# Second mixer's gates and output projections by token in 512 columns, and no filler matmuls at the opening

## The chip, the cores and the metric

One Trainium2 chip, one of its cores. The time is device microseconds of one execution, taken as the median of several runs.

## The reference

Two transformer blocks over 256 tokens of 1024 features, float32, one after the other. What the change touches is the end of the second block's mixer: three branches (a sparse attention `nsa`, a convolution, an attention over a memory), each projected to 1024 features and multiplied by its own gate, summed, and projected once more into the residual:

```python
xn = rms_norm_2(x, norm_mix)
proj = xn @ w_in                      # g_merge: the last 3 * 1024 columns
...
gm = jax.nn.sigmoid(g_merge).reshape(b, s, N_BRANCH, D_MODEL)
merged = gm[:, :, 0] * (o_nsa @ w_nsa_out) + gm[:, :, 1] * (u @ w_conv_out) + gm[:, :, 2] * (o_mem @ w_mem_out)
h = x + merged @ w_out
hn = rms_norm_2(h, norm_ffn)
return h + (silu(hn @ w_gate) * (hn @ w_up)) @ w_down
```

## The kernel before, in words

All weights (150 MB) are streamed once, in 143 chunks of 128x2048 float32 (1 MB). Every chunk passes through a ring of three buffers: SyncE's DMA writes `raw` (after the chunk three before has been split, semaphore `lo_made`), ScalarE casts it to float32r, `whi` (line 1295, `split_hi`, after TensorE has finished the chunk three before, `chunk_used`), VectorE subtracts the rounded from the raw one, `wlo` (line 1873, `split_lo`), and TensorE multiplies. Each product is three matmuls, hi*hi, hi*lo and lo*hi (`mm3`, lines 628 to 630), and the activations are held in two parts too, `hT_hi`/`hT_lo` and `oT_hi`/`oT_lo`. "Feature-major" is a result with features on the partitions and 256 tokens as columns (`feature_major`: weights stationary, activations moving, 256 columns a matmul); "by token" is one with 128 tokens on the partitions and 512 features as columns (`half_of_pair`, `into_residual`: activations stationary, weights moving, 512 columns a matmul). A pair's two halves are the first and last four of eight blocks of the contraction, accumulated in two banks of PSUM.

Each engine runs its own program, a loop over the chunks in which hand-written conditions on the step number `s` (0 at the chunk `kcvc`) say what else is done in that step. ScalarE's step for chunk n is: evacuate chunk n (`evac2`), cast chunk n+3 (`split_hi(n + RING)`, which waits until TensorE has finished chunk n), then pieces of attention. VectorE's is: evacuate an output chunk (`evac2_end`, lines 2237 and 2242), pieces of attention, `split_lo(n + RING)`, then a number of convolution taps given by the list `TAPS_AT` (line 2347). Units are the banks 4 and 5 of PSUM by turns; TensorE waits in `free_unit` until the one it wants has been drained.

The second mixer's chunks in order: `gm0..3` (memory gates), `gn0..3`, `gc0`, `ogn0,1`, `ogm0,1` (output projections, 512 columns each), `gc1..3`, `ogc0,1`, `xout0..3` (`w_out_2`, into the residual). A gate chunk is 256 features, feature-major; ScalarE evacuates it with a tanh (line 1607) once it is finished. An output chunk is feature-major too, in two units, and VectorE multiplies each unit by its gate (line 2237) and adds it to the merged tile `Mg` (line 2242, semaphore `merged`). The merged tile lies as `xout` wants it, so ScalarE (line 1805, `mhi_made`) and VectorE (line 2449, `mlo_made`) only split it in two parts. TensorE's attention pieces stand behind a step's chunk: `att_values(s - 11)`, `att_turn(s - 10)`, `att_scores(s - 8)`. The convolution's layer norm is at steps 26 to 28: sums on TensorE (lines 1230, 1235), the rest on ScalarE (lines 1791 to 1799, 1728 to 1742) and VectorE (lines 2435 to 2442, 2373, 2430).

At the opening TensorE multiplies the identity by itself (`keep_warm`, line 748), 4 matmuls and then 10, with a small transpose of the norm's gains between them (line 922), until the rows of x have been scaled; then `turn_input` (line 772) turns x into feature-major form with 16 matmuls. A float32 matmul of the identity counts as two instructions in the trace.

## Time and profile before

| | |
|---|---|
| median of 3 runs | 910.32 us (910.21 to 910.83) |
| the profiled execution | 910.42 us, its span 908.4 us |
| TensorE busy | 901.1 us, 99% of the span |
| its weight loads | 800.8 us, 88% |
| VectorE, ScalarE, GpSimd | 69%, 57%, 9% |
| granted TensorE clock | 1.00 |
| HBM read | 153.5 MB, 170 GB/s over the span |

Every duration below comes from the profiled execution, whose span begins at 0 and leaves 2.0 us of its time outside. Matmuls overlap their neighbours, so that a chunk's length is read from the start of its first matmul to the start of the next chunk's first. DVE is VectorE, ACT is ScalarE, PE is TensorE and PEld its weight loads.

### The profile page before, as it was taken

The numbers are of one execution on the slowest core, as the hardware profiler recorded it, in microseconds if no ns is written. First come the engines' busy times: TensorE is split into PE (matmuls) and PEld (weight loads), VectorE is DVE, ScalarE is ACT, GpSimd is POOL, SyncE is SP. The second block draws the span as 40 slices with busy tenths as digits, with TensorE's granted clock in tenths as the row PEclk, the third lists the DMA queues.
The fourth block names the chain that finished last, engine by engine and source line by source line (L and its number), as shares of the span: only waits on it lengthen the run. The fifth ranks groups of instructions, "written<-read, shape, count | busy, mean of one in ns | idle before, by whom it ended". The sixth has DMA issues, their size and how long they took to land.

```text
span 908.4 us, 14119 instructions
## 1 busy us (share of the span) xinstructions
PE 901.1 (99%) x5682; PEld 800.8 (88%) x5682; DVE 629.4 (69%) x805; ACT 518.6 (57%) x731; POOL 78.4 (9%) x145
## 2 busy tenths in 40 slices
PE   8999999999999999999999999999999999999998
PEld 7888888999989888888889988888999888888887
DVE  5646576766776666566685889888878586666664
ACT  6646666765455444444476777877365564444441
POOL 8603342020010000000000000000000000000000
PEclk9999999999999999999999999999999999999999
DMA  9654333466545555555555863433445475556541
GB/s 275 219 188 159 114 123 108 142 225 212 181 163 168 204 185 185 185 186 189 200 149 166 259 189 100 139 124 110 139 140 185 139 230 188 185 186 193 187 173 46
DMA packets 115672, 155.35 MB, mean 171 GB/s; under 512 B 2649, under 2 KB 94913, under 8 KB 115618
## 3 DMA queue, kind: packets, MB, share of 16 engines
q1 hardware_dynamic: 114704, 151.57, 51.4%
q0 software_dynamic: 864, 2.98, 1.0%
q8 instruction: 39, 0.64, 0.3%
q14 instruction: 15, 0.12, 0.0%
q10 hardware_dynamic: 50, 0.04, 0.0%
HBM read 153.53 MB, written 1.05 MB: 170 GB/s over the span
## 4 chain that ended last, share of the span: by engine, by line
PE 95%; ACT 2%; DVE 2%; issue 1%; DMA 0%; ACTq 0%; DVEq 0%
PE PS L628 19%; PE PS L629 18%; PE PS L630 18%; PE PS L987 15%; PE PS L992 8%; PE PS L681 3%; PE PS L687 1%; PE PS L1123 1%; PE PS L1101 1%; PE PS L891 1%; ACT whi L1295 1%; PE PS L1035 1%; DVE wlo L1873 1%; PE PS L1159 1%; PE PS L842 1%
## 5 line engine op out<-in xcount | busy, mean ns | idle before, releaser
L1873 DVE TENSOR_TENSOR wlo<-raw,whi 128x2048 fp32r<-128x2048 f32 x141 | 323.8, 2297 | 124.5 <-ACT whi L1295 123.1
L1295 ACT CAST whi<-raw 128x2048 fp32r<-128x2048 f32 x141 | 269.0, 1908 | 112.7 <-PE PS L630 109.5
L628 PE MATMUL PS<-hT,whi 128*128 128x256 f32 (+1 forms) x504 | 145.2, 288 | 0.0
L987 PE MATMUL PS<-hT,whi 128*128 128x512 f32 x608 | 144.7, 390 | 0.0
L630 PE MATMUL PS<-hT,wlo 128*128 128x256 f32 (+1 forms) x504 | 142.5, 283 | 0.0
L629 PE MATMUL PS<-hT,whi 128*128 128x256 f32 (+1 forms) x504 | 142.5, 283 | 0.0
L987 PEld LDWEIGHTS PS<-hT,whi 128*128 128x128 f32 x608 | 113.1, 188 | 23.1 <-issue 0.2
L628 PEld LDWEIGHTS PS<-hT,whi 128*128 128x128 f32 (+1 forms) x504 | 96.0, 190 | 0.7 <-DVE wlo L1873 0.4
L629 PEld LDWEIGHTS PS<-hT,whi 128*128 128x128 f32 (+1 forms) x504 | 96.0, 191 | 0.2
L630 PEld LDWEIGHTS PS<-hT,wlo 128*128 128x128 f32 (+1 forms) x504 | 96.0, 190 | 0.0
L628 PE MATMUL PS<-whi,aT_hi 128*128 128x512 f32 x216 | 84.3, 391 | 0.0
L629 PE MATMUL PS<-wlo,aT_hi 128*128 128x512 f32 x216 | 84.3, 390 | 0.0
L630 PE MATMUL PS<-whi,aT_lo 128*128 128x512 f32 x216 | 84.0, 389 | 0.0
L992 PEld LDWEIGHTS PS<-hT,wlo 128*128 128x128 f32 x608 | 78.0, 191 | 3.0
L992 PE MATMUL PS<-hT,wlo 128*128 128x256 f32 x608 | 78.9, 283 | 0.0
L628 PE MATMUL PS<-oT_hi,whi 128*128 128x256 f32 x224 | 64.1, 286 | 1.0 <-DVE AR L2142 0.5
L629 PE MATMUL PS<-oT_lo,whi 128*128 128x256 f32 x224 | 63.4, 283 | 0.0
L630 PE MATMUL PS<-oT_hi,wlo 128*128 128x256 f32 x224 | 63.4, 283 | 0.0
L628 PE MATMUL PS<-whi,hT 128*128 128x512 f32 (+1 forms) x160 | 61.7, 386 | 0.0
L630 PE MATMUL PS<-whi,hT 128*128 128x512 f32 (+1 forms) x160 | 60.7, 379 | 0.0
L629 PE MATMUL PS<-wlo,hT 128*128 128x512 f32 (+1 forms) x160 | 60.6, 379 | 0.0
L2347 DVE SCALAR_TENSOR_TENSOR AR<-AR,cw 128x256 f32<-128x256 f32 x120 | 49.0, 480 | 0.1
(381 smaller groups left out, 1342.9 us busy)
## 6 DMA issues: line engine op xcount, KB each, us to landing
raw<-in_w_in_dram SPq DMA_DIRECT2D x47, 1024.0 KB, 5.2
raw<-in_w_ff_dram SPq DMA_DIRECT2D x32, 1024.0 KB, 5.2
raw<-in_w_gate_dram SPq DMA_DIRECT2D x11, 1024.0 KB, 5.2
raw<-in_w_up_dram SPq DMA_DIRECT2D x11, 1024.0 KB, 5.3
raw<-in_w_down_dram SPq DMA_DIRECT2D x11, 1024.0 KB, 5.0
raw<-in_w_out_dram SPq DMA_DIRECT2D x8, 1024.0 KB, 5.0
raw<-in_w_proj_gla_dram SPq DMA_DIRECT2D x4, 1024.0 KB, 5.1
raw<-in_w_mem_kv_dram SPq DMA_DIRECT2D x4, 1024.0 KB, 5.1
```

The costliest lines, as they stand in the source:

```text
L628: pe.matmul(dst, a_hi, b_hi, start=start, stop=False, skip_group_check=True)
L629: pe.matmul(dst, a_hi, b_lo, start=False, stop=False, skip_group_check=True)
L630: return pe.matmul(dst, a_lo, b_hi, start=False, stop=stop, skip_group_check=True)
L681: pe.matmul(PS[:, b + c, :], w_hi[:, k, c * P:(c + 1) * P], hT[:, k, :, :].rearrange("p w t -> p (w t)"), start=k == 0, stop=False, skip_g ...
L687: mm = pe.matmul(PS[:, b + c, 0:T], w_lo[:, k, c * P:(c + 1) * P], hT_hi[:, k, :], start=False, stop=k == KT - 1, skip_group_check=True)
L842: pe.matmul(PS[:, b, 0:384], negtri[:, :], sbt[:, b, 1, :], start=False, stop=False, skip_group_check=True)
L891: pe.matmul(o, QK[:, l, :], q, start=True, stop=True)
L987: pe.matmul(PS[:, bank + c, :], w_hi[:, k, c * P:(c + 1) * P], hT[:, k, :, :].rearrange("p w t -> p (w t)"), start=k == 0, stop=False, ski ...
L992: mm = pe.matmul(PS[:, bank + c, 0:T], w_lo[:, k, c * P:(c + 1) * P], hT_hi[:, k, :], start=False, stop=k == KT - 1, skip_group_check=True)
L1295: act.copy(whi[:, n % RING, :], raw[:, n % RING, :]).then_inc(hi_made, 1)
L1873: dve.tensor_tensor(wlo[:, n % RING, :], raw[:, n % RING, :], whi[:, n % RING, :].bitcast(F32), ALU.subtract).then_inc(lo_made, 1)
L2347: ins = dve.scalar_tensor_tensor(cacc[:, f, :], src, cw[:, f, k:k + 1], cacc[:, f, :], ALU.mult, ALU.add)
```

## The change

The twelve gate chunks become six pairs by token (`gm0`+`gm1` and so on; each half is now 512 features and half of the contraction), `gc1` moves from behind `ogm1` to directly behind `gc0`, the gates are laid out by token in other places, and the first of a pair is evacuated at the end of ScalarE's step, once the second half of the pair has finished its first bank. Output chunks are computed by token (`out_by_token`). The merged tile is now by token, so TensorE turns it (`turn_merged`, 8 transposes in the middle of `ogc1`, 8 behind `xout0`), into banks 6 and 7, from which ScalarE (`merged_hi`) and VectorE (`merged_lo`) take their parts. `keep_warm` and its two calls go. The diff, with the declarations and the tables of loads cut:

```diff
     for name in ("gm", "gn"):
-        for c in range(4):
-            gate_chunk(name, c)
-    gate_chunk("gc", 0)
+        for c in (0, 2):
+            gate_pair(name, c)
+    gate_pair("gc", 0)
     for name in ("gn", "gm"):
             out_chunk(name, c)
-    for c in range(1, 4):
-        gate_chunk("gc", c)
+    gate_pair("gc", 2)
     for c in range(2):
...
-            c = int(name[2])
-            if name[1] == "m":
-                return Mg[:, 2 * c:2 * c + 2, :]
-            c = c - 1 if name[1] == "c" else c
-            flat = AR[:, 8312:8824] if c < 0 else AR[:, 7800:8312] if c == 3 else relu[:, c, :]
-            return flat.rearrange("p (f t) -> p f t", f=2)
+            kind, j = name[:2], int(name[2])
+            if kind == "gm":
+                return xn[:, j % 2, 512 * (j // 2):512 * (j // 2) + 512]
+            if kind == "gn":
+                return relu[:, j, :] if j < 3 else AR[:, 7800:8312]
+            return (AR[:, 8312:8824], AR[:, 5120:5632], relu[:, 1, :], relu[:, 2, :])[j]
...
         units_before_ffn1 = unit_of["vm0"]
-        FIRST_OF_PAIR = ("sbv0", "gv0", "gout0", "gv2", "gout2", "vm0")
-        SECOND_OF_PAIR = ("sbv1", "gv1", "gout1", "gv3", "gout3", "vm1")
+        GATES = [f"{kind}{c}" for kind in ("gm", "gn", "gc") for c in range(4)]
+        FIRST_OF_PAIR = ["sbv0", "gv0", "gout0", "gv2", "gout2", "vm0"] + GATES[0::2]
+        SECOND_OF_PAIR = ["sbv1", "gv1", "gout1", "gv3", "gout3", "vm1"] + GATES[1::2]
         TWO_BANKS = [name for name in at if name.startswith(("projs", "o")) or name in SECOND_OF_PAIR]
...
-            def keep_warm(bank, count):
-
-                for _ in range(count):
-                    pe.matmul(PS[:, bank, 0:P], ident[:, :], ident[:, :], start=True, stop=True)
-
             def transposes(event, q, src):
...
             pe.wait_ge(ident_made, 4)
-            keep_warm(7, 4)
             pe.wait_ge(prm0_in, 16)
             pe.transpose(PS[:, 5, 0:8], prm_rows[0:8, :], ident[0:8, 0:8]).then_inc(prm_tr, 1)
-            keep_warm(7, 10)
             pe.wait_ge(prm0_made, 1)
...
+            def turn_merged(c):
+
+                pe.wait_ge(merged, 4 + 2 * c + 2)
+                if c == 1:
+                    pe.wait_ge(mlo_made, 2)
+                for f in range(4):
+                    for a in range(TT):
+                        mm = pe.transpose(PS[:, 6 + f // 2, f % 2 * T + a * P:f % 2 * T + (a + 1) * P],
+                                          xn[:, a, 512 * c + f * P:512 * c + (f + 1) * P], ident[:, :])
+                    if f % 2 == 1:
+                        mm.then_inc(mtr_made, 1)
+
+            def out_by_token(name, k0):
+
+                n, u = at[name], unit_of[name]
+                take(n)
+                w_hi, w_lo = parts(n, 512)
+                for a in range(TT):
+                    if (name, a) == ("ogc1", 1):
+                        turn_merged(0)
+                    free_unit(u + a)
+                    for k in range(4):
+                        mm = mm3(lin(u + a), oT_hi[:, k0 + k, a * P:(a + 1) * P], oT_lo[:, k0 + k, a * P:(a + 1) * P],
+                                 w_hi[:, k, :], w_lo[:, k, :], k == 0, k == 3)
+                    if a == 0:
+                        mm.then_inc(bank_full, 1)
+                mm.then_inc(chunk_used, 1)
+
             B2 = at["kcvc"]
...
                             pe.wait_ge(att_lo, 4)
-                    feature_major(name, oT_hi, oT_lo, (8, 4, 0)[br], 4, 512)
+                    out_by_token(name, (8, 4, 0)[br])
+                elif name in GATES:
+                    half_of_pair(name, hT_hi, hT_lo)
                 else:
...
                               start=c == 0, by_token=c == 3)
+                if c == 0:
+                    turn_merged(1)
             turn_sums()
...
                 n, u = at[name], unit_of[name]
-                if name == "vm0":
-                    act.wait_ge(bank_full, TWO_BANKS.index("vm1") + 1)
+                if name in FIRST_OF_PAIR:
+                    act.wait_ge(bank_full, TWO_BANKS.index(f"{name[:2]}{c_of(name) + 1}") + 1)
                 else:
...
                 elif name[0] == "g":
-                    if name in ("gc1", "gc2", "gc3"):
+                    if name in ("gc2", "gc3"):
                         act.wait_ge(merged, c_of(name))
-                    act.activation(gate_tile(name), two, ACT.Tanh, scale=0.5).then_inc(done, 1)
+                    act.activation(gate_tile(name), lin(u), ACT.Tanh, scale=0.5).then_inc(done, 1)
                 elif name[:2] == "cg":
...
+            def merged_hi(c):
+                for q in (2 * c, 2 * c + 1):
+                    act.wait_ge(mtr_made, q + 1)
+                    act.activation(hT_hi[:, 2 * q:2 * q + 2, :], PS[:, 6 + q % 2, :].rearrange("p (f t) -> p f t", f=2),
+                                   ACT.Copy, scale=0.5).then_inc(mhi_made, 1)
+
             V1 = at["vm0"]
...
                     turned_hi(3, hT_hi, G_MIX2)
-                if name[0] != "o" and name not in ("vm0", "wk0", "wv0"):
+                if name[0] != "o" and name not in FIRST_OF_PAIR and name not in ("wk0", "wv0"):
                     evac2(name)
...
                     tables(EXP_TANH)
-                if name in ("ogc0", "ogc1"):
-                    c = int(name[3])
-                    for i in range(2):
-                        act.wait_ge(merged, 4 + 2 * c + i + 1)
-                        q = 2 * c + i
-                        act.activation(hT_hi[:, 2 * q:2 * q + 2, :], Mg[:, 2 * q:2 * q + 2, :], ACT.Copy,
-                                       scale=0.5).then_inc(mhi_made, 1)
+                if name in GATES and name in FIRST_OF_PAIR:
+                    evac2(name)
+                if name == "ogc1":
+                    merged_hi(0)
+            merged_hi(1)
             for c in range(3):
...
                             dve.wait_ge(chunk_used, at[name] + 1)
-                        f = slice(4 * c + 2 * i, 4 * c + 2 * i + 2)
                         d = drained[(u + i) % 2]
-                        two = lin(u + i).rearrange("p (f t) -> p f t", f=2)
-                        m, t = Mg[:, f, :], gate_tile(f"{name[1:3]}{2 * c + i}")
+                        m, t = gate_tile(f"gm{2 * c + i}"), gate_tile(f"{name[1:3]}{2 * c + i}")
                         g = m if name[2] == "m" else t
-                        dve.scalar_tensor_tensor(g, g, 1.0, two, ALU.add, ALU.mult).then_inc(d, 1)
+                        dve.scalar_tensor_tensor(g, g, 1.0, lin(u + i), ALU.add, ALU.mult).then_inc(d, 1)
                         if name[2] == "n":
...
+            def merged_lo(c):
+                for q in (2 * c, 2 * c + 1):
+                    dve.wait_ge(mhi_made, q + 1)
+                    dve.scalar_tensor_tensor(hT_lo[:, 2 * q:2 * q + 2, :], PS[:, 6 + q % 2, :].rearrange("p (f t) -> p f t", f=2),
+                                             0.5, hT_hi[:, 2 * q:2 * q + 2, :].bitcast(F32), ALU.mult,
+                                             ALU.subtract).then_inc(mlo_made, 1)
+
             def taps_by(s):
...
                 evac(name)
+                if name == "ogc1":
+                    merged_lo(0)
                 if name[0] == "o":
...
                                              ALU.mult).then_inc(cv_y, 1)
-                if name in ("ogc0", "ogc1"):
-                    c = int(name[3])
-                    for i in range(2):
-                        q = 2 * c + i
-                        dve.wait_ge(mhi_made, q + 1)
-                        dve.scalar_tensor_tensor(hT_lo[:, 2 * q:2 * q + 2, :], Mg[:, 2 * q:2 * q + 2, :], 0.5,
-                                                 hT_hi[:, 2 * q:2 * q + 2, :].bitcast(F32), ALU.mult,
-                                                 ALU.subtract).then_inc(mlo_made, 1)
+            merged_lo(1)
             for c in range(2):
```

Three places where instructions move. In the rows, a tile's name stands left of the arrow where it is written, and the names in brackets are the semaphores waited for; line numbers are each kernel's own.

ScalarE at the end of the mixer, before: the evacuations of `gc2` and `gc3` (relu), the casts of whi for `ogc1`, `xout0`, `xout1`, `xout2`, `xout3` and the chunk behind it, and the two pairs of copies that split the merged tile (xn).
```order
L1607 ACTIVATE relu<-PS 128x512 [waits merged,chunk_used]
L1295 CAST whi<-raw 128x2048 [waits chunk_used,landed0]
L1607 ACTIVATE relu<-PS 128x512 [waits merged,chunk_used]
L1295 CAST whi<-raw 128x2048 [waits chunk_used,landed1]
L1295 CAST whi<-raw 128x2048 [waits chunk_used,landed2]
L1805 ACTIVATE hT<-xn 128x2x256 [waits merged] x2
L1295 CAST whi<-raw 128x2048 [waits chunk_used,landed0]
L1805 ACTIVATE hT<-xn 128x2x256 [waits merged] x2
L1295 CAST whi<-raw 128x2048 [waits chunk_used,landed1]
L1295 CAST whi<-raw 128x2048 [waits chunk_used,landed2]
```
And now (the second row is the cast for `ogc1`; the three rows ahead of the copies are the casts for `xout0`, `xout1` and `xout2`):
```order
L1771 ACTIVATE oT_hi<-AR 128x1024 [waits cv_f]
L1319 CAST whi<-raw 128x2048 [waits chunk_used,landed0]
L1631 ACTIVATE relu<-PS 128x512 [waits merged,bank_full]
L1631 ACTIVATE relu<-PS 128x512 [waits merged,chunk_used]
L1319 CAST whi<-raw 128x2048 [waits chunk_used,landed1]
L1319 CAST whi<-raw 128x2048 [waits chunk_used,landed2]
L1319 CAST whi<-raw 128x2048 [waits chunk_used,landed0]
L1738 ACTIVATE hT<-PS 128x2x256 [waits mtr_made] x4
L1319 CAST whi<-raw 128x2048 [waits chunk_used,landed1]
L1319 CAST whi<-raw 128x2048 [waits chunk_used,landed2]
```
All four copies now stand together behind the third of these casts, and they wait for TensorE's turning; before, the first two stood ahead of it.

VectorE where the taps end, before: the taps of steps 23, 24 and 25 (`gc0`, `ogn0`, `ogn1`), with the gate products of `ogn0` and `ogn1` (relu and AR) between them.
```order
L2347 SCALAR_TENSOR_TENSOR AR<-AR,cw 128x256 [waits taps] x7
L2237 SCALAR_TENSOR_TENSOR relu<-relu,PS 128x512 [waits bank_full]
L2237 SCALAR_TENSOR_TENSOR relu<-relu,PS 128x512 [waits chunk_used]
L1873 TENSOR_TENSOR wlo<-raw,whi 128x2048 [waits hi_made]
L2320 TENSOR_TENSOR oT_lo<-PS,oT_hi 128x4x128 [waits att_hi]
L2347 SCALAR_TENSOR_TENSOR AR<-AR,cw 128x256 [waits taps] x6
L2237 SCALAR_TENSOR_TENSOR relu<-relu,PS 128x512 [waits bank_full]
L2237 SCALAR_TENSOR_TENSOR AR<-AR,PS 128x512 [waits chunk_used]
L1873 TENSOR_TENSOR wlo<-raw,whi 128x2048 [waits hi_made]
L2347 SCALAR_TENSOR_TENSOR AR<-AR,cw 128x256 [waits taps] x5
L2237 SCALAR_TENSOR_TENSOR xn<-xn,PS 128x512 [waits bank_full]
```
And now, steps 23 to 26 (`gc0`, `gc1`, `ogn0`, `ogn1`):
```order
L2373 SCALAR_TENSOR_TENSOR AR<-AR,cw 128x256 [waits taps] x7
L1901 TENSOR_TENSOR wlo<-raw,whi 128x2048 [waits hi_made]
L2346 TENSOR_TENSOR oT_lo<-PS,oT_hi 128x4x128 [waits att_hi]
L2373 SCALAR_TENSOR_TENSOR AR<-AR,cw 128x256 [waits taps] x6
L2263 SCALAR_TENSOR_TENSOR relu<-relu,PS 128x512 [waits bank_full]
L2263 SCALAR_TENSOR_TENSOR relu<-relu,PS 128x512 [waits chunk_used]
L1901 TENSOR_TENSOR wlo<-raw,whi 128x2048 [waits hi_made]
L2373 SCALAR_TENSOR_TENSOR AR<-AR,cw 128x256 [waits taps] x5
L2263 SCALAR_TENSOR_TENSOR relu<-relu,PS 128x512 [waits bank_full]
L2263 SCALAR_TENSOR_TENSOR AR<-AR,PS 128x512 [waits chunk_used]
```
The six taps stood behind the products of `ogn0`; they now stand ahead of them, in the step of `gc1`.

TensorE at the opening, before:
```order
L748 MATMUL PS<-ident 128x128 [waits ident_made]
L748 MATMUL PS<-ident 128x128 x3
L922 MATMUL PS<-ident,AR 128x8 [waits prm0_in]
L748 MATMUL PS<-ident 128x128 x10
L772 MATMUL PS<-AR,res 128x128 [waits rdiag_made,prm0_made]
L772 MATMUL PS<-AR,res 128x128 x5
L772 MATMUL PS<-AR,res 128x128 [waits rdiag_made]
L772 MATMUL PS<-AR,res 128x128 x9
L628 MATMUL PS<-hT,whi 66x256 [waits trlo_made,lo_made]
```
And now:
```order
L915 MATMUL PS<-ident,AR 128x8 [waits prm0_in,ident_made]
L766 MATMUL PS<-AR,res 128x128 [waits rdiag_made,prm0_made]
L766 MATMUL PS<-AR,res 128x128 x5
L766 MATMUL PS<-AR,res 128x128 [waits rdiag_made]
L766 MATMUL PS<-AR,res 128x128 x9
L627 MATMUL PS<-hT,whi 66x256 [waits trlo_made,lo_made]
```
The two runs of the identity are gone; what stands behind them waits for the same semaphores as before.

## Rows read from the trace of the kernel before

**Rows 1.** The page, part 1: busy us (share of the span) and instructions of each engine
```profile
PE 901.1 (99%) x5682; PEld 800.8 (88%) x5682; DVE 629.4 (69%) x805; ACT 518.6 (57%) x731; POOL 78.4 (9%) x145
```

**Rows 2.** Waits of TensorE over the whole span: us in total, times, longest us
```profile
PE PS L628 <- DVE AR L2142: 0.5, 1, 0.5
PE PS L628 <- DVE relu L2237: 0.5, 1, 0.5
```

**Rows 3.** Timeline of TensorE, first matmuls of ogc0, ogc1, xout0, xout1 (start us, us)
```profile
686.99 0.28 PE L628 MATMUL PS<-oT_hi,whi 128*128 128x256 f32 x1
...
692.75 0.28 PE L628 MATMUL PS<-oT_hi,whi 128*128 128x256 f32 x1
...
698.51 0.40 PE L628 MATMUL PS<-whi,hT 128*128 128x512 f32 x1
...
703.98 0.39 PE L628 MATMUL PS<-whi,hT 128*128 128x512 f32 x1
```

**Rows 4.** Busy us (and instructions) of PE, PEld, DVE, ACT, POOL, gm1 to gc0
```profile
568.47:638.04 69.57, 69.57 (x545) 62.03 (x544) 59.73 (x125) 53.41 (x117) 0.00 (x0) 1.00 0.41 129
```

**Rows 5.** Timeline of TensorE, eight transposes inside the first block (start us, us)
```profile
247.71 1.04 PE L756 MATMUL PS<-ident,AR 128*128 128x128 f32 x8
248.51 0.47 PE L628 MATMUL PS<-whi,hT 128*128 128x512 f32 x1
```

**Rows 6.** Timeline of ScalarE after the end of ogc1
```profile
698.77 1.92 ACT L1295 CAST whi<-raw 128x2048 fp32r<-128x2048 f32 x1 [2.80 <-PE PS L630]
700.58 0.62 ACT L1805 ACTIVATE hT<-xn 128x512 fp32r<-128x512 f32 x1
```

**Rows 7.** Timeline of VectorE, during ogc1
```profile
697.16 1.28 DVE L2449 SCALAR_TENSOR_TENSOR hT<-xn,hT 128x512 fp32r<-128x512 f32 x2
```

**Rows 8.** The chain of waits, 640 to 720 us (start us, us, what)
```profile
646.55 1.91 ACT whi L1295
648.48 2.29 DVE wlo L1873
...
651.37 2.37 DVE AR L2347 x6
653.75 0.61 DVE relu L2237
654.49 0.36 PE PS L628
...
668.15 1.73 PE PS L1235 x8
```

**Rows 9.** Timeline of ScalarE after the end of gc0
```profile
638.08 0.60 ACT L1607 ACTIVATE AR<-PS 128x512 f32<-128x512 f32 x1 [1.35 <-PE PS L630]
638.57 1.89 ACT L1295 CAST whi<-raw 128x2048 fp32r<-128x2048 f32 x1
```

**Rows 10.** Timeline of TensorE, between ogn0 and ogn1
```profile
646.29 1.95 PE L1142 MATMUL PS<-TMP,AR 128*128 128x128 f32 x16
648.00 0.36 PE L628 MATMUL PS<-oT_hi,whi 128*128 128x256 f32 x1
```

**Rows 11.** Timeline of VectorE, the convolution after ogm1
```profile
673.78 1.22 DVE L2442 SCALAR_TENSOR_TENSOR AR<-AR 128x1024 f32<-128x1024 f32 x1
```

**Rows 12.** Timeline of TensorE, opening (start us, us)
```profile
1.91 2.08 PE L748 MATMUL PS<-ident 128*128 128x128 f32 x8 [1.91 <-POOL eps L520]
...
4.12 3.29 PE L748 MATMUL PS<-ident 128*128 128x128 f32 x20
7.89 3.81 PE L772 MATMUL PS<-AR,res 128*128 128x128 f32 x32 [0.47 <-DVE AR L2079]
```

**Rows 13.** The same, two pieces of the fillers, merged by narrower windows
```profile
4.49 1.47 PE L748 MATMUL PS<-ident 128*128 128x128 f32 x6
...
5.91 1.50 PE L748 MATMUL PS<-ident 128*128 128x128 f32 x12
```

**Rows 14.** Timeline of VectorE, opening
```profile
7.18 0.55 DVE L2079 TENSOR_SCALAR AR<-ident,stat 128x128 f32<-128x128 f32 x1
```

More of the change, by code:

```diff
@@ L91, in key_chunk, with gate_pair @@
         chunk(name, cols(w_in_2, 768, 512).rearrange("p k (b h n) -> p k b h n", b=2, h=2)[:, :, :, c, :])
-    def gate_chunk(name, c):
-        chunk(f"{name}{c}", cols(w_in_2, {"gm": g20, "gc": g10, "gn": g00}[name] + CW * c))
+    def gate_pair(name, c):
+        pair(name, w_in_2, {"gm": g20, "gc": g10, "gn": g00}[name], c)
     def out_chunk(name, c):
@@ L268, in two_block_kernel @@
         hwork = AR[:, 9150:9210]
-        Mg = xn[:, :, :].rearrange("p a (f t) -> p (a f) t", t=T)
         fsq, qsq = xn[:, 0, 0:512], xn[:, 0, 512:1024]
@@ L344, in two_block_kernel @@
                              "cv_sig", "cv_f", "cv_hi", "cv_lo"))
-        merged, mhi_made, mlo_made = sem("merged"), sem("mhi_made"), sem("mlo_made")
+        merged, mtr_made, mhi_made, mlo_made = sem("merged"), sem("mtr_made"), sem("mhi_made"), sem("mlo_made")
         act_link = sem("act_link")
```

## The prediction

> **What bounds the kernel now.** I read the page first: TensorE is busy 901.1 of 908.4 us [rows 1]. Then its idle time: 1.9 us before the first instruction and 0.5 before the turning of x [rows 12]; the two largest waits after the opening are 0.5 us each [rows 2]. So the time is the sum of TensorE's work, and a change counts in three ways: shorter work, added work, and new waits for the other engines. In the third view, the busy times of the stretch with gates and attention, VectorE has 59.7 and ScalarE 53.4 of 69.6 us [rows 4]; they keep up with little to spare, so their order has to be read too. Last I read the opening in the timeline. What a measurement of this kernel can tell from no change is taken as 0.2%, 1.8 us.
>
> **Shorter work.** Twelve gate chunks and six output chunks of the second mixer go from 48 matmuls of 256 columns to 24 of 512. An old chunk lasts 5.76 us, from the first matmul of ogc0 to that of ogc1 and again to xout0; xout0, which already has 24 matmuls of 512, lasts 5.47 [rows 3]. Eighteen times 0.3 is 5.2 to 5.8 us; I take **-5.6**, as xout0's length contains one slow start. The widest bound below would be nothing gained, which the equal product of columns (48 x 256 = 24 x 512) would allow; the rows 3 exclude it.
>
> **Added work.** Two times eight transposes of the merged tile. Eight of the same size cost 0.80 us up to the next matmul, which then takes 0.08 more than usual [rows 5]. Twice 0.9 is **+1.8** (1.6 to 2.1).
>
> **New wait before xout0.** TensorE used to read the split of a tile that was merged long before. Now the chain is transposes in PSUM, ScalarE's copy, VectorE's subtraction, xout0. The order of ScalarE (shown above) has both pairs of copies behind the cast of xout2, and that cast waits until ogc1 is finished, since it writes the buffer that ogc1 reads. So from the moment at which xout0 starts today (698.51) nothing is hidden: 0.26 until the cast starts, 1.81 from there to the next instruction, a copy 0.62 [rows 3, 6], 0.03 until VectorE takes it, one of the two subtractions 0.68 [rows 7], and 0.15 from VectorE's end to TensorE's start, as from 7.73 to 7.89 [rows 12, 14]. Sum 3.55, with 0.05 for a slow first matmul **+3.6** (3.0 if the hand-overs overlap, 4.2 if reading PSUM is slower). The eight transposes themselves stand before ogc1's second half, where they need ogc0's merge; by the same steps that is ready about 1 us early. The second turn stands after xout0 and has its whole 5.4 us for VectorE's four merge operations, and xout1 is between it and its reader: nothing.
>
> **New wait at ogn1.** The chain of waits shows that the old order is already tight in one place: after ogn0 the cast (646.55), the subtraction, six taps (651.37) and VectorE's read of ogn1's bank (653.75) end only at 654.49, where TensorE had waited 0.50 us [rows 8, 2]. That cast to that read is one step. Now the step belongs to gc1, which is the second of its pair, so ScalarE first evacuates it, 0.49 us ahead of the cast [rows 9]; and the bank that VectorE reads behind the taps is ogn0's, which ogn1 needs. From the end of gc1: 0.04 until ScalarE begins, 0.49, and 7.94 (646.55 to 654.49) = 8.5 us until ogn1 may start. TensorE arrives after 1.71 us of memory attention [rows 10] and ogn0's 5.45: 7.2. It waits 1.3; the old 0.5 goes. **+0.8** (0.3 to 1.3).
>
> **New wait at gc2.** The convolution's normalisation ran beside a gate chunk; now it runs beside ogm1, an output chunk, whose first bank VectorE reads only behind it. VectorE is through at 675.00, 6.85 us after 668.15 [rows 8, 11]; plus 0.61 and 0.15 is 7.6. TensorE needs 1.73 for its sums [rows 8] and 5.45: 7.2. A wait also costs the overlap of two neighbouring matmuls, so **+0.4** (0 to 0.6).
>
> **The rest of the mixer.** The first half of a gate pair is evacuated in the middle of the second, so both banks of a pair come free before the next pair only if ScalarE has by then left the attention's exponentials. Its work per step is only moved from the start of a step to its end, and two evacuations follow each other where the pair ends; the next pair starts behind 2 to 4 us of attention matmuls. VectorE's idle time in that stretch, 9.8 us [rows 4], absorbs the 0.3 us that each step gets shorter. I count nothing, with 1 us as the upper bound if that cover goes. DMA sees the same bytes and stands ahead of the casts.
>
> **The opening.** The fillers run from 1.91 to 7.4 us; the turning of x starts at 7.89 and waits for VectorE's 7.18 + 0.55, not for them [rows 12, 14]. Removing them frees no time. But six passes of the filler from 4.49 on last 1.47 us, twelve from 5.91 on only 1.50 [rows 13]: less one pass's own 0.40 and 0.28, that is 0.213 against 0.111 us each, so TensorE left its lower level (1.2 GHz) for the upper (2.4 GHz) at about 5.8, after 3.9 us of fillers. (The granted clock reads 1.00 in every row; here the pace tells.) The turning of x, 32 passes in 3.81 us, ran wholly at the upper level. Without fillers TensorE stands still until 7.9 but for one tiny transpose. If the level follows the work, 3.9 us at the lower level give 3.9 x (1 - 0.111/0.213) = **+1.9**; nothing hides it, as TensorE never waits for long later. Bounds: nothing, if the level rises with time and not with work; 2.6, if it needs as much as the whole 5.5 us that the fillers gave it. One rise cannot tell which.
> The Trainium skill ("TensorE: Matmul & The Clock Gate", What's actually happening) says that the throttled state is the default and that activity releases it. By that rule the opening costs its 1.9 us and the total is the forecast; by the other reading the total is rival 1.
>
> **Sum.** -5.6 + 1.8 + 3.6 + 0.8 + 0.4 + 1.9 = +2.9 us, against the profiled execution's 910.4 (span 908.4): 913.3, span 911.3. The median of the runs is 0.1 below the profiled one: **913.2 us**, 0.32% slower.
>
> **Rivals.**
> 1. The opening is free: the clock would have risen by then anyway. For: the trace shows one rise only. Against: the engine was working whenever it rose. 910.3 + 1.0 = 911.3, no measurable change. It decides once the opening costs under 0.8 us.
> 2. The clock falls in the 3.6 us before xout0. The trace has no such idle stretch once TensorE is warm, so nothing in it excludes this. Coming back would cost once more what the fillers needed, 1.9: 915.1.
> The Trainium skill warns of just that (same page, Why this matters for your kernels): an idle gap between bursts of matmuls puts the gate back to half. No stretch of this trace shows it.
> 3. Faster: the copies of the merged tile reach ScalarE before ogc1 ends. Copy, subtraction and hand-overs, 1.5 us, then hide behind ogc1's second half of 2.7, and the wait before xout0 is gone: with a free opening 910.3 - 5.6 + 1.8 + 0.8 + 0.4 = 907.7, with the opening paid 909.6. It decides when that wait is under 0.8 us and the opening free. Against it stands ScalarE's order, which a trace can hardly contradict.
> 4. TensorE outruns ScalarE and VectorE all along the gates, each pair waiting for its banks, say 0.5 us for each of six pairs: 3 us more, 916.2.
>
> **Chances.** Forecast 0.60, rival 1 0.18, rival 2 0.10, rival 3 0.08, rival 4 0.04. The forecast's own spread puts 0.09 of its 0.60 below 912.1, and of rival 3 0.03 are with the opening paid, 909.6. Slower by over 0.2%: 0.51 + 0.10 + 0.04 = 0.65. Within 0.2% (908.5 to 912.1): 0.09 + 0.18 + 0.03 = 0.30. Faster: 0.05. The range for 8 in 10 reaches from rival 1 (911.3, less 0.4 for its terms) to rival 2 (915.1): 910.9 to 915.3. All bounds together give 909.4 (-5.8 + 1.6 + 3.0 + 0.3) to 916.9 (-5.2 + 2.1 + 4.2 + 1.3 + 0.6 + 1.0 + 2.6).
>
> **What would show it.** In the changed kernel's profile: gate and output chunks 5.45 apart; TensorE's waits list VectorE's subtraction ahead of xout0 with about 3.4 (counted from the end of the matmul before), VectorE's gate product ahead of ogn1 with 1.3 and of gc2 with 0.3; turning x takes 5.7 us instead of 3.8. I am wrong if the turning of x lasts 3.8, if the wait before xout0 is under 1, if the matmuls of xout0 are twice as long as before, or if TensorE waits for ScalarE's gate evacuations.

## The result, and the profile after

The changed kernel takes 914.92 us in the median of 5 runs (914.28 to 917.20), the kernel before 910.32 in the 5 runs beside it (910.11 to 911.83): a ratio of 1.0052, with a 95% interval of 1.0040 to 1.0064. It is 4.6 us slower, where 2.9 were forecast. Measured a second time (the last experiment) it was 6.0 slower, which is outside the forecast's range. The profiled execution took 914.28 us, span 912.5, so 4.1 more span than before.

The page of the changed kernel, part 1, which answers to [rows 1]:

```profile
span 912.5 us, 13226 instructions
PE 896.0 (98%) x5238; PEld 776.4 (85%) x5238; DVE 629.8 (69%) x805; ACT 519.1 (57%) x731; POOL 72.6 (8%) x145
```

TensorE's work fell by 5.1 us and the span grew by 4.1, so 9 us of new idle time have to be found. They stand in TensorE's waits of the changed kernel (for what it waited, us in total, times, longest; PS L766 <- DVE AR L2107 is a write to PSUM in line 766 that waited for VectorE's write to AR in line 2107); compare [rows 2]:

```profile
PE PS L766 <- DVE AR L2107: 3.8, 1, 3.8
PE PS L915 <- DMA AR<-in_norm_mix_dram: 3.3, 1, 3.3
PE PS L627 <- DVE hT L2380: 3.3, 1, 3.3
PE PS L627 <- DVE relu L2263: 1.2, 1, 1.2
PE PS L627 <- DVE AR L2170: 0.5, 1, 0.5
PE PS L627 <- DVE xn L2263: 0.4, 1, 0.4
```

The first two rows are the opening, where fillers used to run. The third is the new wait ahead of `xout0`, the fourth the one at `ogn1`, the sixth the one at `gc2`. The 0.5 is an old wait in the first mixer.

**The wait ahead of `xout0`.** Timelines of the changed kernel (start us, us, engine, line, operation, count, and in brackets the idle time before it and what ended it), first of ScalarE:

```profile
696.97 1.90 ACT L1319 CAST whi<-raw 128x2048 fp32r<-128x2048 f32 x1 [4.76 <-PE PS L629]
698.77 1.08 ACT L1738 ACTIVATE hT<-PS 128x512 fp32r<-128x512 f32 x2
```

of VectorE:

```profile
699.40 1.29 DVE L2380 SCALAR_TENSOR_TENSOR hT<-PS,hT 128x512 fp32r<-128x512 f32 x2 [4.86 <-ACT hT L1738]
```

and of TensorE:

```profile
696.49 0.39 PE L629 MATMUL PS<-whi,oT_lo 128*128 128x512 f32 x1
700.14 0.80 PE L627 MATMUL PS<-whi,hT 128*128 128x512 f32 x1 [3.26 <-DVE hT L2380]
700.74 0.63 PE L628 MATMUL PS<-wlo,hT 128*128 128x512 f32 x1
701.16 0.63 PE L629 MATMUL PS<-whi,hT 128*128 128x512 f32 x1
...
703.51 0.40 PE L629 MATMUL PS<-whi,hT 128*128 128x512 f32 x1
703.75 0.40 PE L627 MATMUL PS<-whi,hT 128*128 128x512 f32 x1
```

ScalarE stood idle for 4.76 us in front of a cast that could not start until `ogc1` had ended, and the two copies that `xout0` needs stood behind that cast: the chain of the prediction, link by link. Two things more are in these rows. The first matmuls of `xout0` are 0.42 us apart, the later ones 0.23. And the windows of the changed kernel (PE, PEld, DVE, ACT and POOL busy; then the granted clock, the DMA share and GB/s) show why:

```profile
690.00:697.00 7.00, 6.82 (x33) 5.26 (x32) 4.39 (x5) 1.95 (x2) 0.00 (x0) 1.00 0.58 200
697.00:700.20 3.20, 0.06 (x1) 0.06 (x1) 0.80 (x2) 2.85 (x3) 0.00 (x0) 0.94 0.62 219
700.20:703.20 3.00, 3.00 (x7) 2.42 (x8) 2.93 (x5) 0.00 (x0) 0.00 (x0) 0.50 0.00 0
703.20:707.00 3.80, 3.80 (x18) 3.05 (x18) 2.33 (x2) 0.00 (x0) 0.00 (x0) 1.00 0.07 12
```

Behind 3.26 us in which TensorE did nothing, the granted clock is 0.50 (1.2 GHz) for three microseconds of full work. That is rival 2, to which the prediction had given 0.10. It is also one of the prediction's own signs of being wrong, the matmuls of `xout0` twice as long as before: up to 703.28 they are nearly that, with 0.41 to 0.43 us from one start to the next (0.60 behind the very first) against 0.23.

**The chunks.** First matmuls of `gc3`, `ogc0` and `ogc1`, and the two turnings of the merged tile, in the changed kernel; compare [rows 3, 5]:

```profile
679.16 0.39 PE L627 MATMUL PS<-whi,hT 128*128 128x512 f32 x1
...
684.60 0.39 PE L627 MATMUL PS<-whi,oT_hi 128*128 128x512 f32 x1
...
690.27 0.47 PE L627 MATMUL PS<-whi,oT_hi 128*128 128x512 f32 x1
...
693.08 1.04 PE L1164 MATMUL PS<-ident,xn 128*128 128x128 f32 x8
...
707.18 1.03 PE L1164 MATMUL PS<-ident,xn 128*128 128x128 f32 x8
707.97 0.48 PE L627 MATMUL PS<-whi,hT 128*128 128x512 f32 x1
```

`gc3` lasts 5.44 (684.60 - 679.16) instead of 5.76. The eight transposes hold TensorE for 0.79 (707.18 to 707.97).

**The opening.** TensorE in the changed kernel, against [rows 12]:

```profile
3.27 0.24 PE L915 MATMUL PS<-ident,AR 8*128 8x8 f32 x1 [3.27 <-DMA AR<-in_norm_mix_dram]
7.35 5.23 PE L766 MATMUL PS<-AR,res 128*128 128x128 f32 x32 [3.84 <-DVE AR L2107]
12.34 0.36 PE L627 MATMUL PS<-hT,whi 128*66 128x256 f32 x1
```

The turning of x begins 0.5 earlier and lasts 5.2 instead of 3.8 us. The clock's column doesn't show why, but the number of matmuls in two windows of 2 us does (11 and 19, with the column at 1.00 in both):

```profile
8.00:10.00 2.00, 2.00 (x11) 2.00 (x11) 1.27 (x4) 0.53 (x1) 1.76 (x4) 1.00 1.10 349
10.00:12.00 2.00, 2.00 (x19) 2.00 (x18) 0.75 (x2) 1.33 (x4) 1.62 (x6) 1.00 1.09 346
```

A good mark for what the whole opening costs is the matmul behind the 0.5 wait in the first mixer, because everything up to it is the same work: 213.37 before, here 214.31.

```profile
214.31 0.36 PE L627 MATMUL PS<-oT_hi,whi 128*128 128x256 f32 x1 [0.51 <-DVE AR L2170]
```

So of the 4.1 us of span 0.9 are the opening and 3.2 the second mixer.

### The profile page after: what moved, and what is told of

Same layout as the page of the kernel before. It is cut to its first block, busy times and chain, and to the rows that moved or that the text cites. A ratio compares the mean times of both kernels' runs of the same rounds, so it can differ in the third digit from the quotient of the medians.

```text
span 912.5 us, 13226 instructions
## 1 busy us (share of the span) xinstructions
PE 896.0 (98%) x5238; PEld 776.4 (85%) x5238; DVE 629.8 (69%) x805; ACT 519.1 (57%) x731; POOL 72.6 (8%) x145
## 4 chain that ended last, share of the span: by engine, by line
PE 94%; ACT 3%; DVE 2%; issue 1%; DMA 0%; ACTq 0%; DVEq 0%
PE PS L627 18%; PE PS L629 18%; PE PS L628 18%; PE PS L979 15%; PE PS L984 8%; PE PS L680 3%; PE PS L686 1%; ACT whi L1319 1%; PE PS L1115 1%; PE PS L1093 1%; PE PS L885 1%; PE PS L1027 1%; DVE wlo L1901 1%; PE PS L1151 1%; PE PS L766 1%
## 5 line engine op out<-in xcount | busy, mean ns | idle before, releaser
L627 PE MATMUL PS<-whi,hT 128*128 128x512 f32 (+1 forms) x256 | 100.9, 394 | 3.7 <-DVE hT L2380 3.3
L629 PE MATMUL PS<-whi,hT 128*128 128x512 f32 (+1 forms) x256 | 98.7, 386 | 0.0
L628 PE MATMUL PS<-wlo,hT 128*128 128x512 f32 (+1 forms) x256 | 98.5, 385 | 0.0
L627 PE MATMUL PS<-hT,whi 128*128 128x256 f32 (+1 forms) x312 | 90.1, 289 | 0.0
L628 PE MATMUL PS<-hT,whi 128*128 128x256 f32 (+1 forms) x312 | 88.2, 283 | 0.0
L629 PE MATMUL PS<-hT,wlo 128*128 128x256 f32 (+1 forms) x312 | 88.2, 283 | 0.0
L627 PEld LDWEIGHTS PS<-whi,hT 128*128 128x128 f32 x256 | 48.5, 190 | 13.3 <-DVE hT L2380 3.7
L627 PEld LDWEIGHTS PS<-hT,whi 128*128 128x128 f32 (+1 forms) x312 | 59.2, 190 | 0.6 <-DVE wlo L1901 0.4
L628 PEld LDWEIGHTS PS<-hT,whi 128*128 128x128 f32 (+1 forms) x312 | 59.2, 190 | 0.2
L629 PEld LDWEIGHTS PS<-hT,wlo 128*128 128x128 f32 (+1 forms) x312 | 59.2, 190 | 0.0
L629 PEld LDWEIGHTS PS<-whi,hT 128*128 128x128 f32 x256 | 48.4, 189 | 9.9
L628 PEld LDWEIGHTS PS<-wlo,hT 128*128 128x128 f32 x256 | 48.6, 190 | 8.9
```

What stands on the lines that cost most here:

```text
L627: pe.matmul(dst, a_hi, b_hi, start=start, stop=False, skip_group_check=True)
L628: pe.matmul(dst, a_hi, b_lo, start=False, stop=False, skip_group_check=True)
L629: return pe.matmul(dst, a_lo, b_hi, start=False, stop=stop, skip_group_check=True)
```

## The experiments

Each kernel below is the changed one with the edit shown, unless it says otherwise. "Mark" is that matmul of the first mixer in its profile, less 213.37. The change in the first row has the 5 runs of the kernel before given above. Of the ten kernels below it, the first four ran on one chip beside 21 runs of the kernel before, the next four on another with 28 runs to compare (median 910.57 for both), and the last two on a third beside 15 runs with 911.0. So differences between rows of different groups can be off by some tenths of a us.

| kernel | median us (runs) | ratio, 95% interval | span | mark | waits: `xout0`, `ogn1` |
|---|---|---|---|---|---|
| the change | 914.92 (5) | 1.0052 (1.0040 to 1.0064) | 912.5 | +0.9 | 3.3, 1.2 |
| fillers back | 914.11 (5) | 1.0036 (1.0023 to 1.0050) | 912.4 | +0.6 | 3.3, 1.2 |
| before, without fillers | 912.77 (11) | 1.0022 (1.0013 to 1.0031) | 911.5 | +3.0 | 0, 0.5 |
| copies first | 910.75 (11) | 1.0000 (0.9991 to 1.0009) | 908.7 | +2.1 | 0, 1.2 |
| fill the wait | 914.34 (5) | 1.0041 (1.0028 to 1.0055) | 912.2 | +2.1 | 0.6 + fillers, 1.2 |
| fillers back, copies first | 908.30 (9) | 0.9974 (0.9964 to 0.9984) | 906.7 | +0.1 | 0, 1.2 |
| the same, taps moved | 908.35 (8) | 0.9974 (0.9963 to 0.9984) | 907.0 | +0.6 | 0, 0 |
| fillers back, fill the wait | 911.98 (11) | 1.0015 (1.0006 to 1.0024) | 910.1 | 0.0 | 0.6 + fillers, 1.2 |
| copies first, taps moved | 911.17 (11) | 1.0001 (0.9992 to 1.0010) | 909.5 | +3.1 | 0, 0 |
| the change again | 916.98 (5) | 1.0071 (1.0057 to 1.0085) | 914.2 | +2.3 | 3.3, 1.2 |
| four fillers only, copies first | 911.16 (11) | 1.0000 (0.9991 to 1.0009) | 909.6 | +3.0 | 0, 1.2 |

### Fillers back

```diff
             pe.wait_ge(ident_made, 4)
+            keep_warm(7, 4)
             pe.wait_ge(prm0_in, 16)
...
+            keep_warm(7, 10)
             pe.wait_ge(prm0_made, 1)
```

> The changed kernel with both runs of fillers back at the opening. Theory (each part of the change has its own price): the turning of x runs at the full level again, 32 passes in 3.8 us instead of 5.2, and the profiled span loses the 0.9 us that the opening cost in the profile, up to 3 in executions whose clock rose later; median 912 to 914, about 1.5 us above nothing but the mixer's part (+3.2). Rival (the fillers cost or give nothing, the spread of the changed kernel comes from elsewhere): median unchanged at 914.9, and as wide a spread, 3 us.

It brought only 0.8 us in the median. In its profile the rise of the clock came later than in the profile of before, so the mark is still 0.6 late; the wait ahead of `xout0` and the half level are there as in the change. Its opening, TensorE and then VectorE:

```profile
4.12 4.50 PE L747 MATMUL PS<-ident 128*128 128x128 f32 x20
8.45 3.74 PE L771 MATMUL PS<-AR,res 128*128 128x128 f32 x32
```
```profile
6.90 0.35 DVE L2114 TENSOR_SCALAR AR<-ident,stat 128x128 f32<-128x128 f32 x1
```

The second run of fillers lasts 4.5 us here, against 3.3 in [rows 12], and ends over a microsecond after VectorE has made what the turning needs (7.25). So fillers are not free: when the clock rises late, they hold up the work behind them. In the four profiled kernels with all 14 of them the turning starts at 7.88, 8.09, 8.45 and 8.54. By itself this run could not price the opening; the pairs below do.

### The kernel before, without fillers

```diff
-            keep_warm(7, 4)
...
-            keep_warm(7, 10)
```

> The kernel before without its fillers, nothing else changed. Theory: +0.9 us as in the profile of the changed kernel, to +3 in executions whose clock rises later; median 911.2 to 912.5 and a wider spread than before's own. Rival (clock rises with time, not with work): 910.3 and a turning of x of 3.8 us.

2.2 us slower, and no wait of the second mixer is touched, so the opening is not free: rival 1 falls. The mark is 3.0 late. Of this, 1.3 stand as a new wait among TensorE's waits of this kernel, and the timelines of ScalarE and of SyncE, which issues the transfers, say where it is from:

```profile
PE PS L681 <- DVE AR L1987: 1.3, 1, 1.3
```
```profile
25.82 1.91 ACT L1293 CAST whi<-raw 128x2048 fp32r<-128x2048 f32 x1 [3.69 <-DMA raw<-in_w_in_dram]
```
```profile
19.29 0.39 SPq L466 DMA_DIRECT2D raw<-in_w_in_dram  x1
```

The same cast (of `sbk1`, the fourth chunk after `low`) starts at 22.55 in the kernel before, there too behind the DMA of its weights, which is issued at 17.16:

```profile
17.16 0.39 SPq L466 DMA_DIRECT2D raw<-in_w_in_dram  x1
```

So of the 3.3 us by which the cast is later, 2.1 come from the issue: it waits until VectorE has split the chunk whose buffer it overwrites, and the late opening delays that. The other 1.2 are the transfer, 6.5 us from issue to cast instead of 5.4. The new wait occurs in three of the seven profiled kernels without all 14 fillers (marks 3.0 to 3.1) and not in the other four (0.9 to 2.3). In three of those four the issue is just as late (19.20 to 19.40), but the cast starts at 24.57 to 24.90. What makes the transfer longer in the first three, no run shows.

### Copies first

```diff
+                if name == "ogc1":
+                    merged_hi(0)
                 split_hi(n + RING)
...
-                if name == "ogc1":
-                    merged_hi(0)
             merged_hi(1)
```

> The changed kernel with ScalarE's first pair of copies of the merged tile ahead of the cast of xout2. Theory: transposes done, copy and subtraction take 1.3 us and hide behind ogc1's second half of 2.7, so the wait of 3.3 before xout0 goes, and with it the fall of the clock that follows it (1.5): 4.9 less in the profile, median about 910.2, no TensorE wait on VectorE's subtraction above 0.3. Rival (the wait is set by VectorE's queue or the cast itself comes late for xout2): 2 us or less of it goes, median 912.5 to 913.

The wait ahead of `xout0` is gone, and with it the half level: 4.2 us less than the change, for two lines that change places. The span is 3.8 less with an opening 1.2 later, so the mixer gives back 5.0, where 4.9 were expected. ScalarE and VectorE in this kernel:

```profile
694.91 1.09 ACT L1738 ACTIVATE hT<-PS 128x512 fp32r<-128x512 f32 x2 [1.54 <-PE PS L1164]
698.16 1.92 ACT L1319 CAST whi<-raw 128x2048 fp32r<-128x2048 f32 x1 [2.17 <-PE PS L629]
```
```profile
695.60 1.28 DVE L2380 SCALAR_TENSOR_TENSOR hT<-PS,hT 128x512 fp32r<-128x512 f32 x2
```

The copies now fill idle time of ScalarE, and both subtractions end at 696.88, 1.2 us before `ogc1` does (698.07). The cast is not delayed, because it waits for TensorE in either order. The price of the whole chain was its place in a queue, not its length.

### Fill the wait

```diff
+            keep_warm(3, 12)
             for c in range(4):
                 pe.wait_ge(mlo_made, c + 1)
```

> The changed kernel with 12 matmuls of the identity into an unused bank between ogc1 and xout0, where TensorE waits 3.3 us. They take 24 passes of 0.11, 2.7 us, so the wait for VectorE stays as a rest of about 0.6. Theory (an idle stretch lets the clock fall, at a price of its own): granted clock 1.00 through xout0, xout0 5.5 instead of 7.0 us long, median 1 to 1.5 below the changed kernel, 913.5. Rival (the price is the wait alone and the fall is an accident of the profile): no change, 914.9.

The time between `ogc1` and `xout0` stays as long and the clock stays up. Against copies first, whose mark is the same (+2.1), the span is 3.5 us longer: that is the wait without its effect on the clock. Against the change the median is only 0.6 lower, between what the theory and its rival named, but this profile's opening is 1.1 us later, so these two do not compare well; the kernel with the fillers back and the wait filled does it better.

### Fillers back and copies first

> The change with its two faults undone together: the 14 filler matmuls are back at the opening, and ScalarE's first two copies (hT, the third and fourth gate chunk's part) stand ahead of the cast of xout2. Theory (the terms of the sum stand and add): no wait ahead of xout0, no fall of the granted clock there, the opening at the full level about as early as in the kernel before; what is left is the 18 chunks' saving (about 5.0) against the transposes (1.8) and the waits of 1.2 and 0.4: 908.5 to 909.0, span 906.6 to 907.1, so 1.6 to 2.0 below the kernel before. Rival (the fillers bring nothing where the copies are early): the same as the copies alone, 910.7. Rival (the rise of the clock comes at a moment that the fillers only shift the odds of): between them, 909.3 to 910, with runs spread over 2 us.

908.30 us, 0.26% faster than the kernel before, and the steadiest of all (908.26 to 908.50 in nine runs). The theory's sum holds: the span is in its range and the median 0.2 below. Against copies first alone the fillers are worth 2.45 us: the rival that they bring nothing falls.

### Fillers, copies first, and three taps earlier

```diff
-            TAPS_AT = [0, 0, 0, 0, 2, 2, 2, 0, 0, 0, 6, 5, 8, 6, 7, 8, 8, 8, 8, 11, 8, 9, 8, 7, 6, 5]
+            TAPS_AT = [0, 0, 0, 0, 2, 2, 2, 0, 0, 0, 6, 5, 8, 6, 7, 8, 8, 8, 8, 11, 8, 9, 8, 10, 3, 5]
```

> As the kernel with the fillers back and the copies first, and three taps of the convolution moved one step earlier (10 and 3 in the place of 7 and 6 taps at the steps before the last). Theory (the wait of 1.2 at ogn1 is VectorE's taps standing in front of the subtraction, and VectorE has room one step earlier): the wait goes, 1.2 less than with both undone, 907.3 to 907.8. Rival (VectorE's work in that stretch is one sum, and the wait moves with the taps): the wait of 1.2 appears one step earlier and the time is the same as with both undone.

The rival held in the time: 908.35, no gain. Only the place is another than it named. The wait of 1.2 at `ogn1` is gone, but a new one stands a chunk later, in front of the sums of the convolution's layer norm. TensorE, then VectorE, in this kernel:

```profile
658.00 1.97 PE L1259 MATMUL PS<-AR,negone 128*128 128x256 f32 x8 [0.69 <-DVE AR L2380]
```
```profile
653.59 2.29 DVE L1908 TENSOR_TENSOR wlo<-raw,whi 128x2048 fp32r<-128x2048 f32 x1 [1.31 <-ACT whi L1326]
655.79 2.06 DVE L2380 SCALAR_TENSOR_TENSOR AR<-AR,cw 128x256 f32<-128x256 f32 x5
```

Those sums need the last tap. The last five taps stand, with this edit as without it, behind a subtraction that follows a cast, and the cast starts (651.64) when `ogn0` ends. So they are through no earlier than before, while TensorE, which no longer waits at `ogn1`, arrives earlier and waits 0.7 for them. Against the kernel with fillers back and copies first, `ogn0` is 1.2 shorter and `ogn1` 1.0 longer. Moving taps by one step does not help; whether an earlier step has room for them was not tried.

### Fillers back, and the wait filled

> The change with the fillers back at the opening and 24 fillers of the identity in the wait ahead of xout0, whose wait for the copies stays. Theory (opening, wait and fall of the clock are three separate prices): only the wait itself is left, 3.5 above the kernel with both undone: 912.0 to 912.6; wait plus fillers ahead of xout0 3.4 to 3.7 us, no half level after it. Rival (the fall and the opening are one price, since the total seen in the change was 4.6 and each alone brought only 0.6 to 0.8): 913.5 or more.

911.98 us, 3.7 above the kernel with both undone and with the same opening: that is the price of the wait ahead of `xout0`. The windows of this kernel over the wait and over the start of `xout0` show the clock at its full level throughout:

```profile
695.00:699.20 4.20, 3.62 (x29) 3.26 (x27) 0.74 (x2) 2.88 (x3) 0.00 (x0) 1.00 0.76 247
699.20:702.00 2.80, 2.80 (x12) 2.34 (x13) 2.73 (x5) 0.00 (x0) 0.00 (x0) 1.00 0.00 0
```

The kernel with the fillers back and the wait left empty is 2.1 us slower (914.11). Of these, 0.5 are its later opening and 1.6 the half level: `xout0` lasts 10.6 us there and 9.0 here, wait included.

### Copies first and taps moved, without fillers

> The change with the copies first and the three taps one step earlier, without fillers at the opening. Theory (the fillers are worth what the late rise of the granted clock costs, and that alone): the opening as in the kernel with copies first (rise 10 to 13 us from the start), the rest as with the fillers: 1 to 2 us above the kernel with all three, 908.8 to 909.6, with single runs spread over 2 us. Rival (the opening is free once the waits behind it are gone): the same as with all three, 907.3 to 907.8.

911.17 us, 2.8 above the same kernel with fillers, with runs from 909.1 to 911.7. The theory named 1 to 2, so the opening costs more than it or the prediction's 1.9 allowed; this profile, too, shows the late transfer.

### The change again

> The change itself, unaltered, a second time, for the spread of its runs: with the wait ahead of xout0 worth 3.6 to 3.7, the missing fillers 2.2 to 2.8 and the half level behind the wait 1.5 to 2.1, the sum above the kernel with both undone (908.3) is 915.6 to 916.9, and the first runs of the change gave 914.9 in the middle, with single runs from 914.3 to 917.2. [...] Rival (the three prices add in every run and the first median was a low draw): median 915.8 or more.

The rival held. A late opening and the half level occur together: in this profile the mark is 2.3 late, the turning of x lasts 6.6 us, and the clock is at 0.50 behind the wait. All five runs are above the four lowest of the first measurement. The three prices add: 908.3 + 3.7 + 1.6 + 2.5 = 916.1, between the two measurements of the change (914.92 and 916.98); the median of all ten runs is 916.2. The opening of its profile:

```profile
7.41 6.61 PE L766 MATMUL PS<-AR,res 128*128 128x128 f32 x32 [4.79 <-DVE AR L2107]
```

And two windows behind the wait, in which `xout0` starts at 701.60:

```profile
701.60:702.60 1.00, 1.00 (x4) 0.86 (x5) 1.00 (x2) 0.00 (x0) 0.00 (x0) 1.00 0.00 0
703.00:705.50 2.50, 2.50 (x8) 1.92 (x6) 2.47 (x4) 0.00 (x0) 0.00 (x0) 0.50 0.00 0
```

Here the clock fell only when TensorE had been at work again for over a microsecond; so it did with the fillers back, while in the first profile of the change it was down before `xout0` began.

### Four fillers only

```diff
             keep_warm(7, 4)
...
-            keep_warm(7, 10)
```

(Each filler counts as two passes, so four of them are 8 instructions in the rows; this is the kernel with fillers and copies first, less the ten.)

> The kernel with both undone, but with only the first four fillers (32 passes of them are 8 in the rows; the ten after the turning of the parameters are left out). Theory (what counts is that TensorE works without a gap from 1.9 us on; four fillers end at 4.0 and leave it idle for 3.5 to 4 us until x is scaled): the opening as without any fillers, 910.3 to 911.3, runs spread over 2 us. Rival (that it starts early is enough): 908.3 to 908.8.

911.16 us, as without any: 2.9 above the kernel with all 14, or 2.4 if each is set against the kernel before on its own chip. Starting early brought nothing here, with TensorE idle for 3.3 us between the fillers and the turning of x.

## Why the prediction was right, and where it was not

The direction was right, and five of the six terms of the sum were right within 0.3 us; the sixth, the opening, was priced too low on average, and the case given 0.10 is what happens. That the first measurement still lies inside the range is partly luck: its opening was a cheap one, which made up for 1.0 of the 1.5 us that the half level cost. The second measurement lies outside.

- **Shorter work, -5.6.** Measured 5.35. The nine chunks `gm0` to `gc0` save 2.47 together, 0.25 to 0.30 each, and the nine others 0.32 each by the rows (5.76 to 5.44). The first nine have attention matmuls behind them; that this is why they save less was not tested.
- **Added work, +1.8.** 0.89 in `xout1`, as read from [rows 5], and 1.23 over `ogc0` and `ogc1`, of which 0.2 stand where the one passes to the other (0.06 idle and a slow first matmul at 690.27): 2.1.
- **New wait before `xout0`, +3.6.** 3.26 idle and some 0.3 of slow restart; 3.5 and 3.7 by the two pairs of kernels. Every link is where it was placed. The reading of ScalarE's program order ahead of time gave this, no view of the trace of before did.
- **New wait at `ogn1`, +0.8.** It waits 1.23 and the old 0.5 is gone: +0.7.
- **New wait at `gc2`, +0.4.** 0.42 idle. From the last matmul of `ogm1` (672.80) to the first of `gc3` (679.16) it is 0.7 longer than without a wait (0.23 + 5.44), so the restart costs the rest.
- **The rest of the mixer, 0.** No wait for ScalarE's gate evacuations appears. Rival 4 fell.
- **The opening, +1.9.** In the first profile 0.9, in the second 2.3. By medians of kernels that differ in the fillers alone it is 2.2 (on the kernel before), 2.45 (copies first), 2.4 (wait filled), 2.8 (taps moved) and 2.9 (against four only, other chip); on the change itself 0.8 by its first five runs and 2.1 by all ten. The sign and the mechanism held: the turning of x runs at the lower pace until TensorE has worked for a while. Three things were missing from the term: how late the rise comes differs from profile to profile, the delayed weight transfer adds 1.2 to 1.3 us in some of them, and removing the fillers does free time, up to 1.2 us, where they outlast the scaling of x.
- **Rival 2, +1.9, chance 0.10.** In all three profiles in which the wait stayed empty the clock fell, at 1.5 to 1.6 us each. The step that failed is its weighing. The prediction held that the trace of before has no such idle stretch and so excludes nothing, and then gave the case a tenth. The trace did show the other half: at the opening, after 1.9 us of idle time, the fillers ran at the lower level (0.213 us a pass). The Trainium skill ("TensorE: Matmul & The Clock Gate", Why this matters for your kernels) names this case, an idle gap between bursts; here the gap was 3.26 us, and the trace agrees.
- **Rival 3** is the edit that repairs the change: 907.7 with a free opening, measured 908.3 with the fillers back; 909.6 with the opening paid, measured 910.75. The copies stood behind the cast by the order of ScalarE's program alone, not by their data.

The sum by these figures for the first profile is -5.35 + 2.1 + 3.6 + 0.7 + 0.7 + 1.5 + 0.9 = +4.2, against 4.1 in the span.

## What to carry to other kernels

When a result takes a new way through other engines, write down each engine's own program order around it: whatever stands in front of the new step and waits for the consumer's own progress turns a hidden chain of 1.5 us into an exposed one of 3.6. Price a new wait of TensorE like the 3.3 us here twice, once as idle time and once as the half-speed work behind it. Before removing idle-time fillers, ask what they keep up as well as what they delay: here they delayed the turning of x by up to 1.2 us, and without them the kernel took 2.2 to 2.9 us longer.

## What the runs showed of the hardware

- A gap of 3.26 or 3.27 us in TensorE's work brought the granted clock from 1.00 to 0.50 for some 3 us of the work behind it, in each of three profiles, in one before the work began again, in two 1.2 to 1.5 us after; with 24 passes of fillers and 0.6 us of idle time in the same place it stayed at 1.00 in two of two. Gaps of 1.23 us (at `ogn1`) never showed a fall.
- Without fillers the turning of x took 5.2 to 6.6 us, with the same work starting at 7.35 to 7.41 in each of three profiles (the change, copies first, the change again). The moment of the rise is not fixed by the program. The spans of the runs fit that: they differ by 1.7 to 2.6 us in each of the four kernels without all fillers that have 11 runs, and by 0.3 to 0.9 in the four with all fillers and no half level (the kernel before among them, with 28 runs).
- At the opening the clock's column reads 1.00 also where equal matmuls run at half the pace ([rows 13]: 0.213 against 0.111 us a pass); there the distances between matmuls tell, not the column.
